# Early features, a shorter token shift and paired chunk chains in a two-block transformer kernel

## The reference

```python
p = h @ w_in                         # 2 * 512 gMLP columns, then 1824 for the time mix
y_a = gmlp_spatial_gating(p[..., :512], p[..., 512:1024], ...)
p = p[..., 1024:]
p = p + (token_shift(p) - p) * mu    # token_shift: the token before, zero for the first
r, k, v, wd, ad, gd = split(p)       # 512, 512, 512, 64, 64, 160 columns
decay = exp(-exp(-softplus(-(w0 + tanh(wd) @ w_up)) - 0.5))
a = sigmoid(a0 + ad @ a_up); g = sigmoid(gd) @ g_up
kk = k * k_k / max(norm_of_head(k * k_k), 1e-12)
k = k * (1 + (a - 1) * k_a)
# per head (8 heads of 64), token by token:
#   S = S * decay + (S @ -kk) (kk * a)^T + v k^T ;  y = S @ r
y = group_norm(y) * lnx_g + lnx_b + sum_of_head(r * k * r_k) * v
y_b = y * g
mix = concat([y_a, y_b]) @ w_out
x = layer_norm(ALPHA * x + gt1 * mix); then the feed-forward part
```

## Time and profile before

| | |
|---|---|
| median of 3 runs | 1824.2 us (1823.96 to 1825.3) |
| the profiled execution | 1824.33 us, span 1822.6 us |
| PE busy | 1654.8 us, 91% of the span |
| PEld, DVE, ACT, POOL busy | 71%, 56%, 40%, 11% |
| granted PE clock, mean | 0.967 |
| last projection product to first product with `w_out_2` | 1106.2 to 1363.4 us of the span |

### The profile page before, as it was taken

The page is one execution under the profiler, slowest core; times in us unless marked ns, Lnnn a source line. Parts: engine busy times, 40 slices in busy tenths (PEclk is TensorE's granted clock), DMA queues, the critical chain, the costliest instruction groups (busy, mean ns, idle before and its releaser), DMA issues. The chain is left out here.

```text
span 1822.6 us, 25057 instructions
## 1 busy us (share of the span) xinstructions
PE 1654.8 (91%) x10328; PEld 1302.9 (71%) x10328; DVE 1012.1 (56%) x1650; ACT 726.8 (40%) x1149; POOL 191.8 (11%) x160
## 2 busy tenths in 40 slices
PE   6999988999999999999998995777779899999995
PEld 5777766887787766777887883655647787887884
DVE  4999967766553676574446474444335453333227
ACT  5533356145423676575225334334222522222111
POOL 2433445300100000000050000000000000000000
PEclk9999999999999999999998997999989899999998
DMA  5332233744553222223242321000001332322321
GB/s 189 93 93 81 81 103 106 248 144 139 153 185 116 81 81 70 81 70 115 93 123 88 103 84 43 3 2 2 3 1 58 116 111 91 99 93 81 93 81 46
DMA packets 45649, 166.13 MB, mean 91 GB/s; under 512 B 5264, under 2 KB 5392, under 8 KB 45536
## 3 DMA queue, kind: packets, MB, share of 16 engines
q1 hardware_dynamic: 42912, 155.95, 27.0%
q0 software_dynamic: 2624, 8.59, 1.5%
HBM read 162.42 MB, written 2.10 MB: 90 GB/s over the span
## 5 line engine op out<-in xcount | busy, mean ns | idle before, releaser
L550 PE MATMUL bank<-h_T_hi,weight_hi 128*128 128x512 f32 x1208 | 494.7, 409 | 3.1 <-DVE scratch L1956 1.4
L593 DVE TENSOR_TENSOR weight_lo<-raw,weight_hi 128x1024 fp32r<-128x1024 f32 x184 | 225.6, 1226 | 487.5 <-ACT weight_hi L585 487.5
L585 ACT ACTIVATE weight_hi<-raw 128x1024 fp32r<-128x1024 f32 x241 | 254.4, 1056 | 591.5 <-PE bank L552 585.3
L551 PE MATMUL bank<-h_T_lo,weight_hi 128*128 128x512 f32 x1208 | 480.9, 398 | 0.0
L552 PE MATMUL bank<-h_T_hi,weight_lo 128*128 128x512 f32 x1208 | 480.4, 398 | 0.0
L550 PEld LDWEIGHTS bank<-h_T_hi,weight_hi 128*128 128x128 f32 x1208 | 229.6, 190 | 65.0 <-issue 9.9
L551 PEld LDWEIGHTS bank<-h_T_lo,weight_hi 128*128 128x128 f32 x1208 | 229.4, 190 | 56.2 <-issue 4.8
L552 PEld LDWEIGHTS bank<-h_T_hi,weight_lo 128*128 128x128 f32 x1208 | 228.9, 189 | 55.5
L1959 DVE SCALAR_TENSOR_TENSOR bank<-conv_in,columns,bank 128x512 f32<-128x512 f32 x240 | 181.4, 756 | 8.3
L593 POOL TENSOR_TENSOR weight_lo<-raw,weight_hi 128x1024 fp32r<-128x1024 f32 x57 | 140.3, 2467 | 208.0 <-ACT weight_hi L585 208.0
L551 PE MATMUL bank<-branch_lo,weight_hi 128*128 128x512 f32 x192 | 76.3, 397 | 0.0
(11 more groups left out here) (412 smaller groups left out, 2389.8 us busy)
## 6 DMA issues: line engine op xcount, KB each, us to landing
raw<-in_weights SPq DMA_DIRECT2D x289, 512.0 KB, 3.5
x_in<-in_x SPq DMA_DIRECT2D x4, 512.0 KB, 7.4
x_rows<-in_x POOLq DMA_DIRECT2D x4, 512.0 KB, 4.9
out<-x_rows SPq DMA_DIRECT2D x4, 512.0 KB, 2.6
mem_in<-in_mem POOLq DMA_DIRECT2D x2, 512.0 KB, 9.0
ln_rows<-in_ln_g POOLq DMA_DIRECT2D x4, 256.0 KB, 3.8
ln_rows<-in_ln_b POOLq DMA_DIRECT2D x4, 256.0 KB, 4.5
silu_row<-in_c POOLq DMA_DIRECT2D x1, 512.0 KB, 11.9
```

The costliest lines, as they stand in the source:

```text
L550: pe.matmul(o, lhs[0], rhs[0], start=start, stop=False)
L551: pe.matmul(o, lhs[0], rhs[1], start=False, stop=False)
L585: act.activation(parts[n % SPLIT][0][:, :], raw[u % RAW][:, :], ACT.Copy).then_inc(*weight_hi.up(u))
L593: engine.tensor_tensor(lo[:, :], raw[u % RAW][:, :], view(hi[:, :]), ALU.subtract).then_inc(*ready.up(u))
```

## The change

Four things:

1. The token shift is two operations. ACT writes bank times (1 - mu) straight to the target, DVE adds the token before times mu, read from the bank (511 columns). A bank of `units` is given back by that DVE operation, no longer by ACT's copy.
2. The 15 units come in the order `SHIFT_ORDER`, and the gMLP steps stand in the first units, one per unit. Tanh and sigmoid of the small inputs come at the fifth unit.
3. Features of f 0 and 1 are cut in `features` (7 steps) and `tokens` (2 steps) and threaded through the last nine units, two steps behind each; tokens(1) stand behind the last unit.
4. The rounds are three: chunks(0), chunks(1) with features(2) and then (3); tokens(2) and then (3), chunks(2), chunks(3), states(0), states(1); gate rows; states(2), states(3). The second group LM comes one step later, the diagonal of P_T at level 4 in place of 1, `s_sq` is two tiles.

```diff
+SHIFT_ORDER = (12, 13, 14, 0, 4, 1, 5, 8, 9, 2, 6, 10, 3, 7, 11)
+HEAD_STEPS = {6: 2, 7: 2, 8: 2, 9: 2, 10: 2, 11: 2, 12: 2, 13: 2, 14: 2}
...
-        for n in range(15):
-            feature_unit(pe, ("rwkv", n), unit_bank(pe, ("rwkv", n)), h2_T)
-            if n in (2, 4, 6, 8):
-                t = n // 2 - 1
+        head = head_features(lambda f: pe_features(pe, f), lambda f: pe_tokens(pe, f))
+        for i, n in enumerate(SHIFT_ORDER):
+            feature_unit(pe, ("rwkv", n), units.take(pe, ("rwkv", n), shift_done, n), h2_T)
+            if 2 <= i < 2 + TT:
+                t = i - 2
...
+            head_steps(head, i)
+
+    def feature_banks(f):
+
+        return feature_places if f < 2 else wide
...
         pe.wait_ge(*dve_f.at(f, "K"))
-        for source in range(2):
+
+        def matrices(source):
...
-            yield
+
+        matrices(0)
+        yield
         for level in range(6):
...
+                matrices(1)
+                yield
                 continue
...
-    def rwkv_tasks(f, features, chunks, states):
-        tasks = []
-        if 0 < f <= FW:
-            tasks.append(chunks(f - 1))
-        if f < FW:
-            tasks.append(features(f))
-        if f > 1:
-            tasks.append(states(f - 2))
-        interleave(*tasks)
+    def shift_target(n):
+        if n < 12:
+            return (AR[:, n % 4, 1, :], k_T[:, n % 4, :], v_T[:, n % 4, :])[n // 4]
+        return lora_in[:, :] if n == 12 else gd_T[:, n - 13, :]
+
+    def head_features(features, tokens):
+
+        return itertools.chain(features(0), features(1), tokens(0), tokens(1))
+
+    def head_steps(head, i):
+        for _ in range(HEAD_STEPS.get(i, 0)):
+            next(head, None)
+
+    def rwkv_rounds(features, tokens, chunks, states, gate_rows):
+        interleave(chunks(0), chunks(1), itertools.chain(features(2), features(3)))
+        interleave(itertools.chain(tokens(2), tokens(3)), chunks(2), chunks(3), states(0), states(1))
+        gate_rows(2)
+        interleave(states(2), states(3))
...
-            o = shifted_ring.take(act, n, shift_done, n)
             act.wait_ge(*product.at("rwkv", n))
-            act.activation(o[:, 1:1 + S], units["rwkv", n], ACT.Copy).then_inc(*taken["act"].up("rwkv", n))
...
+            activate(act, shift_target(n), units["rwkv", n], ACT.Copy, scale=spot("one_minus_mu", n=15)[:, n:n + 1]).then_inc(
+                *shift_own.up(n))
...
-            p, change = shifted_ring[n], change_ring.take(dve, n, shift_done, n)
-            dve.wait_ge(*taken["act"].at("rwkv", n))
-            dve.tensor_tensor(change, p[:, 0:S], p[:, 1:1 + S], ALU.subtract).then_inc(*dve_own.up())
...
-            fused(dve, target, change, column("mu_shift_2", n), p[:, 1:1 + S], ALU.mult, ALU.add).then_inc(*shift_done.up(n))
...
+            o, p = shift_target(n), units["rwkv", n]
+            dve.wait_ge(*shift_own.at(n))
+            fused(dve, o[:, 1:S], p[:, 0:S - 1], column("mu_shift_2", n), o[:, 1:S], ALU.mult, ALU.add).then_inc(*shift_done.up(n))
```

More of the change, by code:

```diff
@@ L132, in unit_plan @@
     t(("pv", 0), "w_in_2", MIX)
-    for n in range(15):
+    for n in SHIFT_ORDER:
         f(("rwkv", n), "w_in_2", 2 * MIX + n * P)
@@ L366, in build @@
     ident_2 = second("ident_2", [P, CHUNK], FP32R)
+    Bw_at = second.at
+    Bw = [second(f"Bw{n}", [P, S]) for n in range(2)]
     loose_at = second.at
@@ L372, in build @@
     w_sp = here.pair("w_sp", [P, 4 * P])
-    shifted = [here(f"shifted{n}", [P, 1 + S]) for n in range(2)]
     rows = [here(f"rows{n}", [P, S]) for n in range(4)]
+    here = Map(nc, Bw_at, loose_at)
     wide_mask = here("wide_mask", [P, 2, P])
@@ L386, in build @@
     work = [(here(f"LM{n}", [P, 2, 2, TT, 2 * CHUNK]), *(here(f"{c}{n}", [P, 8, CHUNK]) for c in "XYV")) for n in range(2)]
+    tokens = [[there(f"tok{n}{c}", [P, TT, P]) for c in "abkv"] for n in range(2)]
+    state_at = there.at
     chunk_state = [(there(f"P_T{n}", [P, NC, CHUNK]), there(f"Z{n}", [P, NC, CHUNK])) for n in range(2)]
-    feature = [(there(f"Bw{n}", [P, S]), [there(f"tok{n}{c}", [P, TT, P]) for c in "abkv"]) for n in range(2)]
+    there = Map(nc, state_at, END)
+    f_sq, f_a, f_kk = ([scratch[n], None, scratch[n], None] for n in (2, 1, 6))
+    f_sq[1], f_a[1], f_kk[1] = (there(f"f_{c}1", [P, S]) for c in ("sq", "a", "kk"))
+    f_sq[3], f_a[3], f_kk[3] = scratch[7], here("f_a3", [P, S]), here("f_kk3", [P, S])
     here = Map(nc, H_AT, B_AT)
@@ L1149, in pe_features, with pe_tokens @@
         yield
-        for n, (source, step) in enumerate(((AR[:, f, 0, :], "A"), (f_kk[:, :], "be"), (f_a[:, :], "ke"), (v_T[:, f, :], None))):
-            bank = wide.take(pe, ("tok", f, n), act_f, f, "tok", n)
+    def pe_tokens(pe, f):
+        bank = stats.take(pe, ("bonus", f), dve_f, f, "bonus")
+        pe.wait_ge(*dve_f.at(f, "rk"))
+        pe.matmul(bank, ones_head[:, :], f_sq[f][:, :], start=True, stop=True).then_inc(*pe_f.up(f, "bonus"))
+        for n, (source, step) in enumerate(((AR[:, f, 0, :], "A"), (f_kk[f][:, :], "be"), (f_a[f][:, :], "ke"), (v_T[:, f, :], None))):
+            bank = feature_banks(f).take(pe, ("tok", f, n), act_f, f, "tok", n)
             if step:
                 pe.wait_ge(*dve_f.at(f, step))
+            else:
+                pe.wait_ge(*shift_done.at(8 + f))
             for i in range(TT):
@@ L1171, in chunk_parts @@
         LM, X, Y, V = work[f % 2]
-        A_tok, B_tok, K_tok, V_tok = feature[f % 2][1]
+        A_tok, B_tok, K_tok, V_tok = tokens[f % 2]
         def table(t):
@@ L1831, in act_features @@
             act.wait_ge(*dve_f.at(f - 1, "A"))
-        activate(act, f_logw[:, :], wide["w", f], ACT.Sigmoid, bias=column("w0_2", f)).then_inc(*act_f.up(f, "log_w"))
+        activate(act, f_logw[:, :], feature_banks(f)["w", f], ACT.Sigmoid, bias=column("w0_2", f)).then_inc(*act_f.up(f, "log_w"))
         act.wait_ge(*pe_f.at(f, "a"))
-        activate(act, f_a[:, :], wide["a", f], ACT.Sigmoid, bias=column("a0_2", f)).then_inc(*act_f.up(f, "a"))
-        if f:
-            act.wait_ge(*pe_f.at(f - 1, "bonus"))
-        act.activation(f_sq[:, :], k_T[:, f, :], ACT.Square, scale=column("k_k_2", f)).then_inc(*act_f.up(f, "sq"))
+        activate(act, f_a[f][:, :], feature_banks(f)["a", f], ACT.Sigmoid, bias=column("a0_2", f)).then_inc(*act_f.up(f, "a"))
+        act.wait_ge(*shift_done.at(4 + f))
+        if f == 2:
+            act.wait_ge(*pe_f.at(0, "bonus"))
+        act.activation(f_sq[f][:, :], k_T[:, f, :], ACT.Square, scale=column("k_k_2", f)).then_inc(*act_f.up(f, "sq"))
         yield
@@ L1861, in act_features @@
                 act.wait_ge(*pe_c.at(f - 2, "QY", 1))
-            act.activation(feature[f % 2][1][n][:, :, :], grid(wide["tok", f, n]), ACT.Copy).then_inc(*act_f.up(f, "tok", n))
+            act.activation(tokens[f % 2][n][:, :, :], grid(feature_banks(f)["tok", f, n]), ACT.Copy).then_inc(*act_f.up(f, "tok", n))
             if n % 2:
```

175 lines of the change are left out of this document (84 added, 91 removed).

## The result

| | before | changed |
|---|---|---|
| median | 1824.75 us (1823.96 to 1833.3) | 1745.62 us (1744.23 to 1749.63) |
| ratio | | 0.9576 (95%: 0.956 to 0.9593) |
| span of the profiled execution | 1822.6 us | 1742.5 us |
| granted PE clock, mean | 0.967 | 0.977 |
| last projection product to first with `w_out_2` | 1106.2 to 1363.4 us | 1117.2 to 1283.4 us |

Four and a quarter per cent less. The changed kernel measured once more (changed_again) gave 1745.95 us and a ratio of 0.9577. The forecast was 1752 us, in a range of 1737 to 1775.

The account below looks back on a forecast made before the run. PE was taken to bound the kernel except in a 257.1 us stretch where it idled 81.4. Terms 16 + 64 + 77 + 28 = 185 us there, a gain of 72.1 from 1824.3, gave 1752 us, range 1737 to 1775.

Parts of the forecast that it names:

- likeliest case: Whole kernel: time between 1742 and 1762 us, given a chance of 0.57.
- head: Features 0 and 1 beside the last nine units: 11.0 us added PE work plus 5.0 of waits, 16 us.
- round A: chunks(0), chunks(1), features(2), (3): 59 us of PE work plus 5 of late V and pauses, 64 us.
- round B: tokens(2), (3), chunks(2), (3), states(0), (1): PE work 72 us, pauses 2, states behind each other 3, 77 us.
- round C with gate rows: Gate rows, states(2), states(3): 20.6 us before, plus 2.3 for gate products and 5 for the second states task, 28 us.
- the square of pair 0: Head: PE waits 3.4 us for ACT's sigmoids and square behind that unit's copies; pair 1's wait is 1.6 us.
- the rival of an unhidden head: Head: PE waits for each step, so features of both pairs stay unhidden; 1790 us, chance 0.03.
- my prices: PE work per task at full clock: chunks 27 us, features 5.5 (2.7 in features, 2.8 in tokens), states 6.2.
- late V in A: First paired round: V is late in two places behind DVE's feature steps, 3 us.
- states behind each other in B: Second paired round: states tasks standing behind each other cost 3 us.
- The pauses: Dense ends of chunk tasks: instruction supply stops PE 2 us per paired round, bounds 0 and 4.6.
- The rival of late V in round A: DVE's feature steps make V late at six places, 17 us, giving 1769 us; chance 0.25 for 1762 to 1780.

Follow-up runs that it names:

- shift_alone: Kernel before with only the token shift in two operations, bank given back by DVE: 1823.65 us, ratio 0.9994.
- steps_alone: Kernel before with only the chunk task's steps moved (second LM group later, empty ACT and DVE steps dropped, P_T diagonal at level 4): 1786.98 us, ratio 0.9802.
- single_chains: Changed kernel with early features kept but one chunk chain at a time again and the states tasks unpaired: 1773.07 us, ratio 0.9719.
- six_moves: Changed kernel with six order moves: square one unit later, gate products last, tokens(2) earlier, square before sigmoids, diagonals later, low y_b a step later: 1728.19 us, ratio 0.9477.

## Why the prediction was right, and where it was wrong

**The time.** 1744.2 us in the profiled execution against a forecast of 1752, inside the range and inside the likeliest case. By terms:

| term | forecast | measured |
|---|---|---|
| head | 16 | 16.3 |
| round A | 64 | 62.7 |
| round B | 77 | 72.6 |
| round C with gate rows | 28 | 27.6 |
| sum of the stretch | 185 | 179.2 |

(Head: the last projection product 11.0 us later, 13.0 when the 2.0 us are put back by which the profiled execution of the changed kernel was ahead at 1015 us, before the stretch begins; to this 3.3 us of tokens. These 2.0 us are the other part of the difference. They are not the work of the change as far as the runs tell: every other kept trace is 1.8 to 4.3 us ahead of that of before at this place, also shift_alone, whose median is that of before, and the medians of before range from 1822.3 to 1824.8 us.)

**Head.** The wait for the square of pair 0 was 3.9 us in place of 3.4, that of pair 1 0.5 in place of 1.6. The order of the units, the threaded steps and the room on DVE did what was said; the rival of an unhidden head, 1790, is out.

**Rounds A and B: work and late copies sized too high, pauses too low.** Busy PE time was 56.95 us in A and 68.78 in B, where I had 59.4 and 72. The prices themselves were right where a chunk chain has one other task beside it: at a clock of 1.00, PE was busy 32.61 us with chunks(0) and features(1) in steps_alone, where my prices make 32.5, and 33.16 us with chunks(3) and states(2) in single_chains, where they make 33.2. Where more tasks stand beside each other they are too high: by 2 us already for tokens(3), chunks(2) and states(1) in single_chains (33.99 for 36.0), and in the paired rounds by 2.5 and 3.2. A likely part of the reason lies in the spans: a group of 32 matmuls spans 1.15 us, but where the next group follows at once it starts 0.95 us after the first (1142.66 and 1143.61 us in steps_alone). By this estimate each group that no longer has a wait behind it saves some 0.2 us of busy time, which adding up prices leaves out.

Of the 3 us for late V in A only 1.0 came, and of the 3 us for states behind each other in B nothing that can be seen: PE is idle 3.8 us there, and its pauses are 3.8. The pauses went the other way, 7.3 us in place of 4: 2 per round were taken, 3.5 and 3.8 measured, within the bounds of 0 and 4.6. That the sum is off by 5.8 us only is thus in part luck, errors of both signs.

The page "Runtime: NRT & Kernel Launch" of the Trainium skill says in "Instruction fetch mechanics" that code comes in blocks of 256 instructions and that the passing of a block is mostly hidden. The first half agrees with the spacing of the pauses here, 127 matmuls and 128 loads; the second does not where 256 instructions of PE run in 2.0 us, since pauses of 1.5 to 1.8 us follow.

**The cause of V's waits: wrong.** The failed step is this: "The wait of 0.89 us per copy is covered by the same group of the other chain", taken as what would end the 31.7 us. The late V was described rightly ("DVE had feature work ahead of the copy"), but its cure was put down to the other chain, and the sentence of the change "The second group LM comes one step later" had no term in the sum. steps_alone shows that this moved step, with the empty ones gone from ACT and DVE, takes V from 31.7 to 10.0 us by itself and is worth 36 us, nearly half of the whole, without any pair. The cover is real but smaller: the pairs take V from 9.7 to 1.0 us. The sum came out right all the same, because I took rounds A and B as work plus a few late copies, and it does not matter to that sum which of the two edits makes the copies punctual. The rival of late V in round A (17 us) is out: V's only wait there is 1.0 us.

**The parts, as the runs price them.** In the order steps, then hidden head and regrouped rounds, then pairs: 0.0198, 0.0083 and 0.0143 of the time of before, 36, 15 and 26 us. The order matters: the head alone taken away from the changed kernel costs 21 us, not 15, and the likely reason is that before one of the two features tasks stood beside a chunk chain. The shift is worth nothing.

**Round C.** 27.6 for 28. Two waits were forecast by name, for the diagonals (1.7 us measured) and at the end; the end was 5.2 us of PE idle, and at the lower clock the gate products took 3.75 us in place of 1.88. The mean clock of the round was 0.75. That 7 of the 27.6 us could be had by order alone, as six_moves does, the prediction did not see.

## What to carry to other kernels

Where tasks are interleaved by steps onto in-order queues, compare the step number of each group with that of its copy on every engine: a copy one step behind its product waits for the whole step of another task, at every level, and looks like a busy engine. Price each moved step, also one that seems to be housekeeping, and ask of a large wait first in which place of the queue its releaser stands and only then what could cover it. After a change that fills the middle, look at the ends, where PE idles: there a microsecond of queue order can be worth more than itself, as in round C, where 4.8 us less of idling came with 2.3 us less of busy time.

## What was not expected of the hardware

- PE pauses 1.2 to 1.9 us with nothing awaited once per about 256 of its instructions where these run densely (127 matmuls of 64 columns and 128 loads in 2.0 us, next pause 3.3 to 4.0 us after the last); the first pause of a dense stretch is shorter, 0.4 to 1.0 us. Leaving products out removed a pause per round; 2.8 us of long matmuls among them brought their sum in round A from 3.5 to between 1.7 and 2.4 us. The last two pauses of round B, 3.4 to 3.9 us apart and 1.3 to 1.8 us long, are at the same two lines in every kernel with paired chains and full products.
- The late copies cost more than their own waits. The four rounds with late V had a mean granted clock of 0.94 to 0.96; with V punctual it was 0.96 to 1.00, and 1.00 also in the round that still has a wait of 2.55 us. Of the 31.8 us saved in these rounds 21.7 are the fall of V's waits (31.7 to 10.0 us) and 6.4 the shorter busy time of PE for the same matmuls (152.75 to 146.32 us); other waits are the rest.
